# Clears, one weight load, the residual rows, the last store and dummy matmuls moved or added in a one-core decoder layer step

## The reference, cut to what matters

```python
h = RMSNorm(x)
ua, va, ga, qb, kb, vb, gb = split(h @ w_in, 7)          # each 512 wide
ya = gelu(ua) * (tril(W_s) @ RMSNorm_group(gelu(va)) + b_s)
yb = attend(qb, kb, vb)                                  # 8 heads of 64, ALiBi
ya = RMSNorm(ya) * silu(ga); yb = RMSNorm(yb) * silu(gb)
y  = concat(ya, yb) @ w_out                              # 1024 x 1024
out = x + RMSNorm(y)
# decode: of 16 blocks of 256 cached keys, q . mean(keys) picks the best 3 per head
# and sequence; attention runs over these and the new token
```

## Time and profile before

| | |
|---|---|
| runs | 427.44, 429.88, 431.46 us; median 429.88 |
| the profiled execution's own time | 428.23 us |
| its span | 426.2 us |
| PE / DVE / POOL / ACT busy | 392.1 / 264.5 / 278.9 / 122.2 us |
| moved by DMA | 111.22 MB, 261 GB/s over the span |
| mean granted clock | 0.975 |

### The profile page before, as it was taken

How to read it: one execution, slowest core, us unless ns; L and a number is a source line. 1 busy time by engine, 2 the same in 40 slices (tenths; PEclk the granted TensorE clock), 3 DMA queues, 4 the chain that set the end, 5 groups by cost and what they waited for, 6 DMA issues and landing times. The chain is left out here.

```text
span 426.2 us, 9218 instructions
## 1 busy us (share of the span) xinstructions
PE 392.1 (92%) x2786; PEld 185.7 (44%) x2786; DVE 264.5 (62%) x693; ACT 122.2 (29%) x277; POOL 278.9 (65%) x442
## 2 busy tenths in 40 slices
PE   5695999999999999999899989999599799989993
PEld 3543344434533464444534555354243354434451
DVE  1164369455953697459748985597555965694432
ACT  3310111000220526546634564556032012101010
POOL 5777755476767766857878776887478856674111
PEclk9998899999999999999999999999799899999998
DMA  8999249998799999986997499918999899825221
GB/s 257 401 378 405 73 156 340 347 336 233 274 344 366 209 345 348 325 220 229 313 340 193 146 359 337 300 39 271 402 317 347 182 369 383 172 61 105 71 91 52
DMA packets 78455, 111.22 MB, mean 261 GB/s; under 512 B 45728, under 2 KB 46880, under 8 KB 78408
## 3 DMA queue, kind: packets, MB, share of 16 engines
q0 software_dynamic: 22576, 71.45, 49.4%
q1 hardware_dynamic: 52424, 38.63, 31.8%
q10 hardware_dynamic: 3408, 0.58, 0.7%
HBM read 106.31 MB, written 4.29 MB: 260 GB/s over the span
## 5 line engine op out<-in xcount | busy, mean ns | idle before, releaser
L1102 PE MATMUL PA<-wbuf,hT 128*128 128x512 f32 x384 | 183.5, 616 | 0.0
L926 POOL DMA_INDIRECT K<-in_cache_k,kidx x128 | 132.8, 1038 | 69.9 <-issue 32.8
L743 DVE TENSOR_TENSOR ksum<-K 128x512 f32<-128x512 f32 x128 | 86.1, 689 | 52.3 <-DMA K<-in_cache_k,kidx 43.0
L1102 PEld LDWEIGHTS PA<-wbuf,hT 128*128 128x128 f32 x384 | 70.2, 196 | 76.6 <-issue 75.9
L727 POOL DMA_DIRECT2D V<-in_cache_v x128 | 76.7, 600 | 17.0 <-issue 10.9
L1211 PE MATMUL PA<-wbuf,hT 128*128 128x512 f32 x128 | 59.2, 604 | 0.1
L756 DVE TENSOR_TENSOR ksum<-K,qb 128x128 f32<-128x128 f32 x128 | 41.5, 397 | 2.2 <-DVE selT L1651 1.9
L1227 PE MATMUL GB<-ksum,win 128*32 128x512 f32 x256 | 34.9, 618 | 6.5 <-DVE ksum L743 6.3
L756 POOL TENSOR_TENSOR ksum<-K,qb 128x128 f32<-128x128 f32 x64 | 29.8, 499 | 13.7 <-DVE selT L1651 8.4
L1211 PEld LDWEIGHTS PA<-wbuf,hT 128*128 128x128 f32 x128 | 22.9, 189 | 26.5 <-issue 26.0
L1102 PE MATMUL PA<-hT,wbuf 128*128 128x512 f32 x64 | 29.1, 600 | 0.0
(11 more groups left out here) (223 smaller groups left out, 377.7 us busy)
## 6 DMA issues: line engine op xcount, KB each, us to landing
wbuf<-in_w_in SPq DMA_DIRECT2D x6, 2048.0 KB, 8.9
V<-in_cache_v SPq DMA_DIRECT2D x240, 32.0 KB
V<-in_cache_v POOLq DMA_DIRECT2D x128, 32.0 KB
wbuf<-in_w_out SPq DMA_DIRECT2D x2, 2048.0 KB, 20.3
wbuf<-in_w_in SPq DMA_DIRECT2D x4, 512.0 KB, 8.1
K<-in_cache_k,kidx POOLq DMA_INDIRECT x128, 7.7
qb<-q_rows SPq DMA_DIRECT2D x8, 256.0 KB, 4.5
ya<-in_x_prompt SPq DMA_DIRECT2D x2, 512.0 KB, 6.7
```

Source lines behind the costliest of these rows:

```text
L743: eng.tensor_tensor(ksum[:, n % SUMS, :], K[:, at, 0, :], K[:, at, 1, :], ALU.add).then_inc(s_dsum, 1)
L926: pool.indirect_dma_start(K[:, m % SLOTS, :, :].rearrange("p r w -> p (r w)"), None, k_rows, bass.IndirectOffsetOnAxis(ap=kidx[:, b, n:n + ...
L1102: last = pe.matmul(bank[:, :], lhs, rhs, start=(kc == 0), stop=(kc == KC - 1))
```

## The change

It has seven parts.

1. POOL makes its clears and tables (the 13 clears, `group`, `xs2`) before it waits for the page table.
2. `LOAD_BEHIND[7]` is 6 in place of 5.
3. `res` waits for the last key block of b = 6, and in the planner it has a transfer of its own on "Q", of the first rank; the ranks of values, weights and keys, three starts, three landings and two costs are set anew.
4. PE begins with two dummy matmuls of 128x512 on a cleared `qb`; DVE clears it first.
5. `rs` (the sample's norm) moves from the lane "first" to "sample".
6. DVE adds EPS in its own sum, so that POOL's step at the end is one instruction.
7. The last tile's final step and store are two halves; the second is stored by ACT, behind its sample stores. ACT's last squares write to `yas` in place of `junk`.

```diff
-LOAD_BEHIND = {2: 0, 3: 1, 4: 2, 5: 3, 6: 4, 7: 5, 8: 6}
+RESIDUAL_BEHIND = 6
+LOAD_BEHIND = {2: 0, 3: 1, 4: 2, 5: 3, 6: 4, 7: 6, 8: 6}
...
-                       ("Q", "value key weight")):
+                       ("Q", "residual value weight key")):
...
-            add("PE", "first", ("rs",), 0.3, ("POOL", ("xs",)))
+            add("PE", "sample", ("rs",), 0.3, ("POOL", ("xs",)))
...
-    add("SP", "residual", ("res",), 2.5, ("PE", ("pv", PAIRS - 1, NT - 1)), ("SP", ("vrow", NT)))
+    add("SP", "residual", ("res",), 2.5, ("PE", ("pv", PAIRS - 1, NT - 1)), ("SP", ("vrow", NT)), ("Q", ("k", RESIDUAL_BEHIND, NB - 1)))
+    add("Q", "residual", ("res",), 7.0, ("SP", ("res",)))
...
                 elif kind == "res":
                     sp.wait_ge(s_ptused, PAIRS * NT)
+                    sp.wait_ge(s_k[NB - 1], 16 * (RESIDUAL_BEHIND + 1))
...
+                    if t < NT - 1:
+                        sp.dma_start(y_rows[t], xres[t].rearrange("p a b -> p (a b)")).then_inc(s_store, 16)
+                    else:
+                        sp.dma_start(y_rows[t][:, 0:W], xres[t][:, 0, :]).then_inc(s_store, 16)
...
+            pe.wait_ge(s_clear, 1)
+            for _ in range(2):
+                pe.matmul(GB[:, :], qb[:, 0:P], qb[:, :], start=True, stop=True)
...
             act.wait_ge(s_sout, 1)
             for j in range(2, G):
                 act.dma_start(ys_rows[:, :, j, :], xs2[32 * j:32 * j + B, :, :]).then_inc(s_store, 16)
+            act.wait_ge(s_yo, NT + 1)
+            act.dma_start(y_rows[NT - 1][:, W:D], xres[NT - 1][:, 1, :]).then_inc(s_store, 16)
...
+            dve.memset(qb[:, :], 0.0).then_inc(s_clear, 1)
...
+                    for part in ([slice(0, 1), slice(1, 2)] if t == NT - 1 else [slice(0, 2)]):
+                        dve.scalar_tensor_tensor(out=xres[t][:, part, :], in0=stage[t][:, part, :],
+                                                 scalar=rstd[:, 41 + 2 * t:42 + 2 * t], in1=xres[t][:, part, :],
+                                                 op0=ALU.mult, op1=ALU.add).then_inc(s_yo, 1)
```

More of the change, by code:

```diff
@@ L82, in spj @@
         weights = [("Q", ("w", c))] if c else [("Q", ("w0", x)) for x in range(QUARTERS)]
-        add("PE", "sample", ("spj", c), 1.9, *weights, *([] if c else [("DVE", ("xs",)), ("PE", ("rs",))]))
+        add("PE", "sample", ("spj", c), 1.9, *weights, *([] if c else [("DVE", ("xs",)), ("POOL", ("xs",))]))
         extra = {"k": [("DVE", ("rs",))], "ga": [("DVE", ("spj", 4)), ("SP", ("vns",))],
@@ L122, in make_plan @@
             add("DVE", "first", ("xs",), 0.3, ("PE", ("xs",)))
-            add("PE", "first", ("rs",), 0.3, ("POOL", ("xs",)))
-            add("DVE", "first", ("rs",), 0.2, ("PE", ("rs",)))
+            add("PE", "sample", ("rs",), 0.3, ("POOL", ("xs",)))
+            add("DVE", "sample", ("rs",), 0.2, ("PE", ("rs",)))
     for c in range(len(CHUNKS)):
@@ L194, in out @@
         add("ACT", "evacuate", ("op", t, half), 0.8, ("PE", ("op", t, half)))
-        add("DVE", "out", ("op", t, half), 0.8, ("ACT", ("op", t, half)), ("SP", ("res",)))
+        add("DVE", "out", ("op", t, half), 0.8, ("ACT", ("op", t, half)), ("Q", ("res",)))
         if half == 1:
-            add("POOL", "root", ("op", t, 1), 1.0, ("DVE", ("op", t, 1)))
+            add("POOL", "root", ("op", t, 1), 0.7, ("DVE", ("op", t, 1)))
             add("DVE", "scale", ("opf", t), 1.3, ("POOL", ("op", t, 1)))
@@ L388, in make_plan @@
     return plan
-PLAN_START = {"PE": 3.6, "ACT": 2.8, "DVE": 1.0, "POOL": 6.3, "SP": 18.0, "Q": 12.0}
-LANDED = [(("x", 0), 4.3), (("x", 1), 10.5), (("x", 2), 12.5), (("x", 3), 14.5), (("xs",), 5.5), (("w", 1), 24.0),
+PLAN_START = {"PE": 4.5, "ACT": 3.5, "DVE": 1.0, "POOL": 8.4, "SP": 20.0, "Q": 12.0}
+LANDED = [(("x", 0), 4.3), (("x", 1), 13.2), (("x", 2), 17.5), (("x", 3), 19.5), (("xs",), 6.2), (("w", 1), 24.0),
           (("w0", 0), 5.8), (("w0", 1), 7.2), (("w0", 2), 8.6), (("w0", 3), 10.0)]
@@ L901, in _ @@
             link(pool.tensor_scalar_add(poff[ROWS:P, :], poff[ROWS:P, :], -float(ROWS)))
+            link(pool.memset(one[:, :], 1.0))
+            link(pool.memset(win[:, :], 0.0))
+            link(pool.memset(win[:, 31:32], 1.0))
+            link(pool.memset(g128[:, :], 0.0))
+            for p in range(PAIRS):
+                link(pool.memset(qsc[0:HD, p:p + 1], SCALE / SLOPES[2 * p]))
+                link(pool.memset(qsc[HD:P, p:p + 1], SCALE / SLOPES[2 * p + 1]))
+            pool.memset(selw[:, :], 0).then_inc(s_ones, 1)
+            link(pool.memset(group[:, :], 0.0))
+            for j in range(G):
+                link(pool.memset(group[32 * j:32 * j + 32, j:j + 1], 1.0))
+            pool.memset(xs2[:, :, :], 0.0).then_inc(s_slowz, 1)
             def make_kidx():
@@ L977, in make_constants @@
                 pool.memset(osb[:, :, :], 0.0).then_inc(s_const, 1)
-            def clear_sample_tables():
-                link(pool.memset(group[:, :], 0.0))
-                for j in range(G):
-                    link(pool.memset(group[32 * j:32 * j + 32, j:j + 1], 1.0))
-                pool.memset(xs2[:, :, :], 0.0).then_inc(s_slowz, 1)
             for s in PLAN["POOL"]:
@@ L1456, in _ @@
                         act.wait_ge(*squared[-1])
[L1457 removed]
+                    last = act.activation(yas[:, HD * hh:HD * hh + HD], obs[:, HD * hh:HD * hh + HD], ACT.Square,
                                           scale=rdenw[:, hh:hh + 1], accum_out=msum[:, 34 + hh:35 + hh])
```

23 lines of the change are left out of this document (6 added, 17 removed).

## The result

The change made the kernel slower: 437.57 us median (434.44 to 440.00, four runs) against 429.82 us for the kernel before, measured beside it. The ratio is 1.018, 95% interval 1.009 to 1.027. The forecast was 426.0, with a range of 414 to 433, so the result lies outside the range and on the other side of no change.

The account below looks back on a forecast made before the run. PE (busy 392.1 of 426.2 us) and the decode key chain were both critical; -5.7 (PE's end) + 2.6 (tail) = -3.1 us: span 423.1, profiled time 425.1, median scale 426.8, forecast between them 426.0, range 414 to 433.

Parts of the forecast that it names:

- part 3: Ninth weight load: issued at 327.3 us, lands at 347.6; PE ends at 413.1 instead of 418.8, 5.7 us sooner.
- part 2: Eighth load and residual leave at about 312 us; PE and keys stand 11.8 us early at the selection of b = 6.
- the trough: Between the keys of b = 6 and the next keys' start at 322.6: 11 us, room for 4.4 MB.
- the opening: Clears ahead of the page table: PE gains 7.5 us, the selection chain 6.5; both 7.5 early at 290 us, bounds 3.0 to 9.6.
- Rival (b): SP's queue backs up 8 us at the eighth load; ninth load lands at 355.6, time 433.1 us; chance 0.15.
- Rival (c): At the start PE swaps its wait for DVE for one for keys: 3.0 us instead of 7.5, time 429.6; chance 0.1.
- The dummies at nothing: Two dummy matmuls ahead of the first transposes: between a loss of 0.8 and a gain of 2 us, taken as 0.
- The eighth load out of the seventh sequence's keys: Keys of b = 6 without the 2 MB load among them: 3.6 to 5.2 us less, 4.3 taken.
- The ninth load's wait: PE reaches the sample projection's second half at 340.0, stands 7.6 us until 347.6, then loses 1.9 to a slow clock.
- The tail: From the last tile's end to the end 13.3 us instead of 7.4; net loss 2.6, bounds -1 to +4.
- The rule on rings: One queue drains in ring order, so the ninth load waits for eighth load, residual and fetches left in SP's queue.
- rival (a): Ninth load takes 8 to 10 us, is there at 337, PE does not stop: 415.6 us; chance 0.25.

Follow-up runs that it names:

- run 3: The changed kernel with only the residual's rows issued behind the ninth weight load, the output gain staying ahead of it: 429.32 us, ratio 1.001.
- run 5: The kernel before with only POOL's clears moved ahead of the page table: 428.70 us, ratio 0.997.
- run 8: Dummy matmuls alone in the kernel before: 430.21 us, 1.003; left out of run 1's kernel: 422.92 us, 0.989; left out with the tail also spread: 420.62 us, 0.980.
- run 4: The kernel before with only the eighth weight load and the residual moved behind the seventh sequence's keys: 427.42 us, ratio 0.997.
- run 2: The changed kernel with the whole residual step, output gain included, issued behind the ninth weight load: 439.14 us, ratio 1.025.
- run 1: The changed kernel with the second half of the sample projection put back behind the fourth half tile on PE: 419.99 us, ratio 0.976.
- 10: Run 1's kernel with the last tile's second to fourth quarter spread between the last value products and the sample's last steps: 419.84 us, ratio 0.977.

## Why the prediction was wrong

The forecast span was 423.1 us, and 437.4 came, 14.3 more. Its own chain, from the ninth load on, takes this apart:

| term | forecast | measured | difference |
|---|---|---|---|
| ninth load issued | 327.3 | 331.4 | +4.1 |
| its time to landing | 20.3 | 28.7 | +8.4 |
| landing to the last tile's end | 62.2 | 62.9 | +0.7 |
| last tile's end to the end | 13.3 | 14.4 | +1.1 |

**The step that failed** is in part 3: "The load needs 20 us when it shares with keys and fetches". That size came from two loads with nothing big ahead of them in their queue. The change puts eighth load, residual and gain there, which part 2 had placed in the trough: "They fit, barely". They did not. Part 2 had them leave at about 312; they left at 316.6, and the gain landed at 336.9, 5.5 us behind the ninth load's issue. With the rows taken out of the way the load took 20.2 us (run 3), so the 20.3 was right for a free queue and wrong for this one. Of the 4.1 us of later issue 3.9 are a lead that was not there: the selection of b = 6, which the issue follows, came at 316.70 and not at 312.8 (324.62 - 11.8), because the opening's lead had been given back.

Rival (b), with a chance of 0.15, came closest. Its landing at 355.6 gave 433.1; the landing was at 360.1. It had the right second half, bytes ahead of the ninth load in its queue. Its first half, a slow pace of the fetches, did not happen: the fetches of b = 5 took 27.3 us, as forecast ("some 27 us"). What held back the eighth load instead were the keys, which began 4.8 us later than forecast (284.97 instead of 280.15) and landed at 314.9, and the four gathers `obs` in SyncE's queue (3.29 us, L861, to 316.5). (The 287.65 of the earlier trace rows and the 284.97 of the change are issues of a third block. The first two of each sequence go out earlier, into the two spare slots, at 269.95 and 272.24 in the kernel before, so the forecast calls "first" what is the third. Before and after are read alike.)

Point by point:

- *The opening*: right at its place, wrong in what remained. The wait for VectorE and the slow clock behind it went, and the first selection came at 48.76, with 49.3 forecast. "I let both run 7.5 us early at 290 us" failed. The sixth selection was 2.9 us early, because the third weight load gives the lead back (run 5): the second selection was already only 2.9 us early. The sum asked what is late next only up to the first selection; the next weight load was not looked at. PE's wait of 3.39 us for POOL ahead of 14.56 us, which the prediction's list of idle places leaves out, went as well; other waits took it, and at the second weight load's sample rows PE was level with before (31.82 against 31.96 us). Rival (c) had the effect right at another place.
- *The dummies at nothing*: right in the old order within what the runs can tell (run 8). In the new one they are between nothing and 1.3%, unsettled.
- *The eighth load out of the seventh sequence's keys*: right. Third block's issue to ready took 29.9 us (284.97 to 314.9) where it was 35.6, 5.7 us less with 3.6 to 5.2 forecast. The gap of 4.97 us became one of 2.2, and the clock did not fall behind it. Moved alone, it can't be told from no change (0.997, 0.992 to 1.001, run 4); PE then stands longer for the values.
- *The ninth load's wait*: the right place, the right cause, 13.9 us instead of 7.6. PE reached the step at 346.2 instead of 340.0. That alone would have shortened the wait; the landing moved by twice as much. The slow clock behind the wait cost 1.4 us by the rows from the step to the next half tile (3.34 us, 1.94 in run 2), with 1.9 priced.
- *The tail*: +7.0 us from the last tile's end, with 5.9 forecast for the same stretch. The estimate of the chain was 1.1 short, 0.7 of it at the x64 (2.60 us, 1.9 priced).
- *The rule on rings*, which I cited and gave to the slower rival instead of to the sum: the Trainium skill (DMA: Bandwidth & Descriptors, "Queues, rings and completion order") says that one queue is drained in ring order. The traces agree as far as they go: 18.5 to 22.0 us in the six where residual and gain had landed or stood behind, 22.7 to 28.7 in the six where they had gone out 11 to 15 us before. It deserved to set the size of the term.

What the change gains without the wait was close to the price: with the step moved the ratio is 0.976 (0.969 to 0.982), where rival (a), the load in time, gave 415.6 on a profiled time of 428.2, a ratio of 0.971. The version of run 1 beats both kernels.

## What to carry to other kernels

Before a step that needs a transfer is moved ahead in an in-order engine, work out the landing from what will still be on its way ahead of that transfer in its own queue, not from how long the same transfer took elsewhere. Put the step ahead of work that doesn't need the transfer only if the margin is larger than the scatter of the landing, here up to 6 us. And when a transfer itself is moved back, look at who stands behind its first consumer: here 0.5 MB of gain held up VectorE for 22.5 us, and PE, which needed the key sums behind it, for 11.4.

When an early stage is made faster, follow the lead to the next weight load, not only to the next wait: the same edit was worth 0.3%, not told from nothing, in one order of work and 1.8% in another.

## What the runs showed of the hardware that I had not expected

The change and the kernels of runs 1, 2, 3 and 10 are alike far beyond the second selection, and yet their third load landed after 12.9, 10.7, 11.2, 11.2 and 8.2 us, and the time between the first two selections was 50.2, 47.5, 46.8, 47.0 and 46.1 us. The ninth load, behind the same queue in the change and in runs 1 and 10, landed after 28.7, 23.0 and 25.6. So one trace of a tightly timed stage can be off by some 4 to 6 us.

Two matmuls with nothing to compute at 1.64 us halved the time of the first quarter rows (1.96 against 3.78 us). They took 3.60 us for four rows themselves. The granted clock reads 1.00 over all of these rows, so in this stretch it does not tell rows of 0.9 us from rows of half that. The time did not change, because the next wait took all of it.
